# Front stage: the order of the first transfers, and the place of the context's scale row

## What is computed

```python
mod_x = silu(c)     @ mod_w[l] + mod_b[l]        # 6 rows of 1024: shift, scale, gate, twice
mod_c = silu(c_ctx) @ mod_w[l] + mod_b[l]
hx = rms_norm(x,   norm1_g[l]) * (1 + sc1)  + sh1     # 8 tiles of 128 tokens
hc = rms_norm(ctx, norm1_g[l]) * (1 + sc1c) + sh1c    # 2 tiles of 128 tokens
q, k, v, gf, gb, bv, bg = split(h @ w_in)             # w_in is 1024 x 3584
u = bv * sigmoid(bg)                                  # feeds the convolution
```

## Time and profile before

| what | value |
|---|---|
| median of 3 runs | 3164.01 us (3162.02, 3164.01, 3170.26) |
| span of the profiled execution | 3154.3 us |
| median less the span (what lies around it) | 9.7 us |
| PE busy over the span | 2870.1 us, 91% |
| DVE, ACT, POOL busy | 2085.9, 1459.1, 739.5 us |
| mean granted TensorE clock | 0.960 |
| the front, start to its last matmul | 0 to about 504 us |

### The profile page before, as it was taken

One profiled execution on the slowest core, in us unless ns is written; L12 is line 12 of the kernel. 1 busy time (PEld: TensorE's weight loads), 2 busy tenths in 40 slices (PEclk: granted clock), 3 DMA queues, 4 the chain that ended last, 5 costly groups with the idle time before them and its releaser, 6 DMA issues. The chain is left out here.

```text
span 3154.3 us, 48793 instructions
## 1 busy us (share of the span) xinstructions
PE 2870.1 (91%) x17608; PEld 2341.2 (74%) x17608; DVE 2085.9 (66%) x2424; ACT 1459.1 (46%) x2151; POOL 739.5 (23%) x1243
## 2 busy tenths in 40 slices
PE   6999997789399999999978899999998939999998
PEld 3776686768277777777757788888887838888887
DVE  3576853844677677676754455555554479999997
ACT  2212113532155555555533344444443227777775
POOL 1000002800012122122125655555530001111111
PEclk8999998989699999999989999999999969999999
DMA  6367725443568788788751000000012369999995
GB/s 229 121 210 249 255 86 196 145 176 134 199 236 299 289 297 299 294 295 299 295 177 47 9 9 16 16 16 16 8 68 95 140 239 379 395 399 389 396 401 191
DMA packets 129713, 631.50 MB, mean 200 GB/s; under 512 B 14785, under 2 KB 29249, under 8 KB 70818
## 3 DMA queue, kind: packets, MB, share of 16 engines
q1 hardware_dynamic: 117282, 591.86, 49.5%
q0 software_dynamic: 12288, 37.75, 4.8%
HBM read 563.40 MB, written 66.16 MB: 200 GB/s over the span
## 5 line engine op out<-in xcount | busy, mean ns | idle before, releaser
L1823 DVE TENSOR_TENSOR ex_wlo<-ring,ex_whi 128x2048 fp32r<-128x2048 f32 x384 | 877.2, 2289 | 213.1 <-ACT ex_whi L1752 208.5
L1752 ACT CAST ex_whi<-ring 128x2048 fp32r<-128x2048 f32 x384 | 727.5, 1904 | 295.0 <-PE psum L1717 210.7
L1717 PE MATMUL psum<-ex_whi,ex_xh 128*128 128x512 f32 x1024 | 403.8, 394 | 0.0
L1717 PE MATMUL psum<-ex_whi,ex_xl 128*128 128x512 f32 x1024 | 399.4, 390 | 0.0
L1717 PE MATMUL psum<-ex_wlo,ex_xh 128*128 128x512 f32 x1024 | 398.7, 389 | 0.0
L469 PE MATMUL psum<-fr_whi,fr_hh 128*128 128x512 f32 x560 | 224.5, 403 | 11.9 <-DVE fr_hl L653 10.8
L1717 PEld LDWEIGHTS psum<-ex_whi,ex_xh 128*128 128x128 f32 x1024 | 192.2, 188 | 44.8 <-issue 6.6
L1717 PEld LDWEIGHTS psum<-ex_whi,ex_xl 128*128 128x128 f32 x1024 | 192.2, 188 | 41.0
L1717 PEld LDWEIGHTS psum<-ex_wlo,ex_xh 128*128 128x128 f32 x1024 | 192.4, 188 | 38.6
L469 PE MATMUL psum<-fr_whi,fr_hl 128*128 128x512 f32 x560 | 218.7, 393 | 0.0
L469 PE MATMUL psum<-fr_wlo,fr_hh 128*128 128x512 f32 x560 | 218.0, 391 | 0.0
(11 more groups left out here) (295 smaller groups left out, 5826.2 us busy)
## 6 DMA issues: line engine op xcount, KB each, us to landing
ring<-in_moe_w SPq DMA_DIRECT2D x384, 1024.0 KB, 8.5
fr_raw<-in_mod_w SPq DMA_DIRECT2D x40, 1024.0 KB, 5.4
rec_d<-fr_work SPq DMA_DIRECT2D x72, 256.0 KB, 5.8
fr_raw<-in_ev_w_in SPq DMA_DIRECT2D x14, 1024.0 KB, 5.7
ring<-rec_d SPq DMA_DIRECT2D x10, 1024.0 KB, 15.5
h_d<-ring SPq DMA_DIRECT2D x18, 512.0 KB, 3.0
fr_arena<-in_mod_w SPq DMA_DIRECT2D x8, 1024.0 KB, 12.0
ring<-mod_d SPq DMA_DIRECT2D x15, 512.0 KB, 7.4
```

The source lines that it names most:

```text
L1717: last = nc.tensor.matmul(g.psum[:, 2 + i % 2, :], x[:, 4 * b + k, :], w[n][:, k, :], start=(b == 0 and k == 0 and first == 0), stop=(b == ...
L1752: nc.scalar.copy(whi[m % RING][:, :, :], slot(i)[:, 4 * b:4 * b + 4, :]).then_inc(hi_set, 1)
L1823: nc.vector.tensor_tensor(wlo[n][:, :, :], slot(i)[:, 4 * b:4 * b + 4, :], whi[n][:, :, :].bitcast(F32), ALU.subtract).then_inc(lo_set, 1)
```

## The change

Three groups of edits, all in the front.

On SP, the eight `g0` loads stand ahead of the wait for the memset and of `load_bias(0)`. Tile 2 is asked for right behind `store_mod(0)`, ahead of the wait for that store. In the loop the order is weight piece 2 and tile 3 in s = 0, piece 3 and tile 4 in s = 1, and tile s + 3 in later steps.

On DVE, `low_h(1)` and `scale(2)` are taken out of step 0 and put behind `low_w(1)`, in this order and ahead of `context_a()`.

On ACT, the wait for `a_made >= 3` goes from ahead of the loop into `evacuate(0)`, behind its wait for the products and ahead of its sigmoid.

```diff
                 sp.dma_start(g.ident[:, :], io["ident_d"]).then_inc(g.ident_in, 16)
+                for k in range(KD):
+                    sp.dma_start(g0[k], rows(io["mod_w"], k)).then_inc(g0_in[k], 16)
                 sp.wait_ge(c_zero, 2)
                 load_bias(0)
-                for k in range(KD):
-                    sp.dma_start(g0[k], rows(io["mod_w"], k)).then_inc(g0_in[k], 16)
                 load_x(0)
                 load_raw(0)
                 load_x(1)
                 load_raw(1)
                 store_mod(0)
+                load_x(2)
                 sp.wait_ge(mod_out, 32)
@@
                 for s in range(f.STEPS + 3):
+                    if s < 2:
+                        load_raw(s + 2)
+                    if s + 3 < NT:
+                        load_x(s + 3)
                     for i in f.loads(s):
-                        load_raw(i)
-                    if s + 2 < NT:
-                        load_x(s + 2)
+                        if i >= 4:
+                            load_raw(i)
@@ def evacuate(s), on ACT
                     act.wait_ge(prod, s + 1)
                     if c < 2:
+                        if s == 0:
+                            act.wait_ge(a_made, 3)
                         if s >= 2:
                             act.wait_ge(u_set, s - 1)
                         nc.scalar.activation(sig[s % 2], g.psum[:, bank(s), 256:512], ACT.Sigmoid).then_inc(sig_set, 1)
@@ ACT
                 square(1)
-                act.wait_ge(a_made, 3)
                 for s in range(f.STEPS + 1):
@@ DVE
                 low_w(1)
+                low_h(1)
+                scale(2)
                 context_a()
@@
-                    if s + 2 < NT:
+                    if 0 < s and s + 2 < NT:
                         scale(s + 2)
-                    if s + 1 < NT:
+                    if 0 < s and s + 1 < NT:
                         low_h(s + 1)
```

## The result

| | before | changed | ratio (95% interval) |
|---|---|---|---|
| first set, 9 runs each | 3162.02 us | 3150.66 us | 0.9958 (0.9947 to 0.9970) |
| second set, 21 and 5 runs | 3161.06 us | 3148.36 us | 0.9960 (0.9946 to 0.9974) |
| third set, 14 and 10 runs | 3158.72 us | 3150.56 us | 0.9972 (0.9962 to 0.9982) |

By the first set's ratio it gains 13.3 us (9.5 to 16.8), by the difference of its medians 11.4 us; the mean of the three ratios, 0.9963, is 11.6 us. 11.2 us were forecast. The profiled execution of the changed kernel took 3148.15 us with a span of 3146.4 us, so 1.75 us lie around a span, not 9.7 us. The first profile of before (span 3154.3 us) was thus one of an execution of about 3156 us, a quick one among runs with a median of 3162.

The account below looks back on a forecast made before the run. PE's 10.8 us wait for `low_h`, with tile 1 held behind late tile 2, was taken as the bound; 9.9 us at step 2 plus 1.25 us gave 11.2, span 3143.1 plus 9.7 around it 3152.8 us, range 3149 to 3160.

Parts of the forecast that it names:

- The path and the sum up to step 2: Front, DVE and ACT chain: step 2 at 54.1 instead of 64.04, 9.9 us, with one PE stall of 2.5 us.
- the old clock: Times as in the profile before, with the 1.25 us from issuing `g0` ahead of the bias not yet taken off.
- the table load waits for the wait coded second: ACT, `evacuate(0)`: the sigmoid's table load, 1.30 us, starts only behind `context_a`, as a load at 395.37 behaved.
- the 9.7 us around it: Time outside the span, added to the forecast span of 3143.1 us to give 3152.8 us.
- The step from a gain to "faster": Whole kernel: 0.3%, 9.5 us, taken as what a measurement can tell; faster 0.63, slower 0.04, within 0.3% 0.33.
- Part 1: SP, start of the run: issuing `g0` ahead of the bias gains 1.25 us, bounds 0 and 1.25; bias costs 0.
- The hole's size: PE ahead of step 1: a 10.8 us wait for `low_h`, with step 2 at 64.04 in the profile before.
- Rival 1: PE between steps 1 and 2: the 2.5 us stall lowers the clock, costing 1.7 us, 3154.5 us; chance 0.24.
- gaps of this size: PE at 30 to 40 us: gaps like the 2.5 us stall (busy 7.18 of 10) went with a clock of 0.83.
- Rival 3: Front: tile 3 or the bias lands late; gain 8 to 9.5 us, 3155.5 us; chance 0.11.
- After it PE's waits are small: PE from step 2 to the front's end: waits of 1.2 and 0.8 us, so earlier gains carry through.
- Rival 4: Steps 2 to 9: DVE's lag does not shrink, PE waits for `low_h` each step; 3168.8 us, chance 0.04.

Follow-up runs that it names:

- tiles only: Kernel before with only SP's new order of token tiles and weight pieces, bias first, DVE and ACT as before: ratio 0.9976 (0.9967 to 0.9985).
- `context_a` dosed: Changed kernel with an unused 128x1024 copy on DVE right ahead of `context_a`'s own operation: 14.55 us from `low_w(1)` to step 2, span 3149.9 us.
- `g0` only: Kernel before with only the eight `g0` loads put ahead of the bias: 3160.84 us, timed once, beside a median of 3161.06 us before.
- order only: Kernel before with only DVE's and ACT's new order, SP as before: ratio 0.9995 (0.9986 to 1.0005).
- bias first: Changed kernel with the bias loads ahead of `g0` again: first modulation row at 27.58, 13.97 us from `low_w(1)` to step 2, span 3149.7 us.
- table early: Changed kernel with the sigmoid's table loaded early by a spare-column sigmoid behind `square(1)` on ACT: 11.80 us from `low_w(1)` to step 2, span 3146.0 us.

## Where the prediction was right, and the steps that failed

**The path and the sum up to step 2.** Right. Step 2 was put at 54.1 on the old clock, so 52.85 on the new, and stands at 52.78. The chain came term by term: `low_h(1)` right behind `low_w(1)`, no stall of step 1, `scale(2)`, `context_a`, table load, sigmoid, `gate_u(0)`, `scale(3)`, `low_h(2)`, and one PE wait of 2.49 us where 2.5 were forecast. That the table load waits for the wait coded second, read from one row at 395.37, held in the changed kernel and in two experiments.

**The base of the sum.** The mechanism was right, and the first step that failed is a term of the sum, "the 9.7 us around it". It measures 1.75 us (3148.15 less 3146.4). The other 8 us were not a constant of the kernel but the distance between a quick execution and a median of three, of which one was 3170.26; the median of nine is 3162.02. The forecast of 3152.8 us took over that high base: with the same 11.2 us it would have been 3150.8, beside the 3150.66 measured. The range's lower end, 3149.0, was thus a gain of 13.0 us from the later median and not the 15 us that I meant.

**The step from a gain to "faster".** This failed too. I set 9.5 us as the difference that a measurement can tell from none, gave the medians "an uncertainty of a microsecond or two", and counted most cases as clear of 9.5 us (0.63). The intervals measured reach 3.6, 4.5 and 3.2 us to either side, and none lies clear above 9.5 us: 9.5 to 16.8, 8.2 to 17.1 and 5.7 to 12.0 us. So a gain of 11.2 us could not be expected to stand clear of such a bound. That there is a gain at all is shown three times, once by a ratio that gives only 8.8 us.

**Part 1.** 1.25 us forecast for the first row; 0.9 us where the last `g0` group ran slowly and 1.25 us at the full clock. The bias came in time each time.

**The hole's size.** I took one profile's 22.96 us as the thing removed. The second has 23.96, so the gain from the distances is 9.9 to 10.9 us, where the sum had 9.9, and with part 1's 0.9 to 1.25 us it is 10.8 to 12.1.

**Rival 1, the clock.** It came in one of three profiles of the changed kernel. In the second one step 2 began at 1.2 GHz behind the 2.53 us wait (0.63 us for a matmul at first, 0.39 later), and step 3 came 7.96 us later and not 6.62 (63.79 and 55.83, against 59.40 and 52.78), so the price was 1.3 us; 1.7 were put on it. Its "gaps of this size" in 30 to 40 us was a misreading: PE's gaps there are 1.4 us, 1.2 us and the start of one of 1.5 us, and 2.8 us is their sum.

```profile
55.83 0.79 PE L473 MATMUL psum<-fr_whi,fr_hh 128*128 128x512 f32 x1 [2.53 <-DVE fr_hl L658]
```

**Rival 3, tile 3.** It landed by 45.14, on the old clock 46.5, 3 us later than the 43.5 reckoned: by the order of SP's requests, piece 2 and the context's rows were ahead of it in the queue, which no run here separates. It cost nothing, but not with the room that the rival gave it ("it would have to be 5 us late"). On ACT the table load and the first sigmoid stand behind `square(3)`, so DVE's need at 50.5 is not what counts: ACT was idle for 0.61 us between `square(3)` and the table load (the row at 46.91), and a tile later by more than that would have delayed step 2.

**"After it PE's waits are small", rows 7.** They are not always. 1.2 us before, but 0.9 to 4.8 us over the thirteen other profiles with either order of the tiles. In the third profile of the changed kernel a modulation piece came 3.10 us late, and the clock fell behind it (PE's row took 1.93 us where 1.06 is usual). SP in that profile, the request for the piece:

```profile
342.81 5.12 SPq L351 DMA_DIRECT2D fr_raw<-in_mod_w  x2
```

DVE there, `low_w` of the weight piece ahead of it in the same buffer:

```profile
340.50 2.29 DVE L664 TENSOR_TENSOR fr_wlo<-fr_raw,fr_whi 128x2048 fp32r<-128x2048 f32 x1 [3.66 <-ACT fr_whi L545]
```

And PE there, the product that waited for the piece:

```profile
345.61 1.93 PE L439 MATMUL psum<-fr_raw,fr_sc 128*32 128x512 f32 x8 [3.10 <-DMA fr_raw<-in_mod_w]
```

In the changed kernel's first profile the same rows stood at 341.19, 338.88 (idle 1.46) and 343.30 (wait 0.21): a weight piece that lands 2 us later (it was asked for at 330.23, and at 330.81 in the first profile, so its transfer took longer) makes `low_w` later, and SP asks for the next modulation piece only behind it. Whether the new order makes this more frequent is open: with the old order of the tiles on SP the rest was 452.0 to 452.6 and once 455.0, with the new one 453.0 to 458.5 in ten profiles. Part of the gain may be given back there; four profiles against ten with such a spread don't tell. From what the first pair of profiles shows, 11.3 us at step 2 became 10.2 at the next stage's first matmul (516.35 and 506.16) and 7.9 in the span, while the timed runs have 11.6; the loss behind the front is not shown to belong to the change.

**Rival 4.** Did not come. `low_h(3)` waited 2.25 us for its own `hh`, so DVE's lag was gone in one step, and step 3 followed step 2 by 6.62 us.

```profile
57.77 1.23 DVE L658 TENSOR_TENSOR fr_hl<-psum,fr_hh 128x1024 fp32r<-128x1024 f32 x1 [2.25 <-ACT fr_hh L549]
```

**What stays open** is the difference between the 13.3 us of the first set and 11.2: the interval reaches from 9.5 to 16.8, the other two sets have 12.6 and 8.8, and the profiles 10.8 to 12.1. The spread of the runs is enough for it; no run looks for a further cause.

## What to carry to other kernels

When an engine's queue has the next tile's work ahead of this tile's, a late load of the next tile stalls this one; the load must be asked for early *and* the order must be turned, and here either alone gave 5.8 and 1.0 us of the 10.4. After the repair, follow the whole chain down to the next product: an operation moved off one path (`context_a`) took a wait, a table load and two DVE steps with it, and a preload and one swap took 2.8 us of the distance back. Make the sum of a small change from distances between neighbouring events, with two profiles at least: absolute positions in one profile, and its distance to a median of three runs, carry several us of chance.

## What the runs showed of the hardware

- The granted clock in the first 40 us differs between executions of the same kernel. The four spreads took 3.67 us in six profiles and 5.37 to 6.74 us in eight, and all that follows moves by it. Nothing in the kernel's order tells which it will be.
- Of five gaps of 2.5 to 2.8 us at PE ahead of a step, two were followed by the low clock (the second profile of the changed kernel, and tiles only) and three were not (its first and third profile, and `context_a` dosed). The four gaps of 9.0 to 11.8 us (both profiles of before, `g0` only, order only) were followed by it each time, the three of 0.6 to 1.3 us (bias first, order only at step 2, table early) never.
- The table load of 1.28 us is issued behind the wait that the code has second, and the activation keeps the first one: this is what the load at 395.37 of before shows and the same load shows in all thirteen other profiles (384.79 to 400.10 us), each released by the store, 5.5 us before the activation. In `evacuate(0)` it starts 0.08 us behind the end of `context_a`. The Trainium skill, "ScalarE: Activation LUTs", section "What ACT_TABLE_LOAD costs", counts a drain of 1.38 us besides. From the load's start to the sigmoid there are 1.29 us here, and taking the load off the path gave 1.28 us back, so the trace does not show the drain.
- On DVE a copy of 128x1024 took 0.69 us, where the operation with two tensors and a scalar takes 1.22.
